# RWKV-7 chunk inverse: the transposed inverse of two heads in four is kept in the other half of the partitions

## The reference, cut to what matters

```python
def step(S, inp):
    r_t, w_t, k_t, v_t, a_t, b_t = inp
    sa = jnp.einsum('bhvk,bhk->bhv', S, a_t)
    S = S * w_t[:, :, None, :] + sa[..., None] * b_t[:, :, None, :] + v_t[..., None] * k_t[:, :, None, :]
    y = jnp.einsum('bhvk,bhk->bhv', S, r_t)
```

## Time and profile before

| | us |
|---|---|
| median of 3 runs (lowest to highest) | 1478.87 (1474.42 to 1480.12) |
| the profiled execution's own time | 1475.65 |
| its span | 1473.7 |
| PE busy in the span | 1400.1 (95%) |
| PEld, DVE, ACT, POOL busy | 1151.5, 869.1, 696.3, 39.7 |

### The profile page before, as it was taken

One profiled execution on the slowest core, in us unless ns is written; L12 is line 12 of the kernel. 1 busy time (PEld: TensorE's weight loads), 2 busy tenths in 40 slices (PEclk: granted clock), 3 DMA queues, 4 the chain that ended last, 5 costly groups with the idle time before them and its releaser, 6 DMA issues.

```text
span 1473.7 us, 22686 instructions
## 1 busy us (share of the span) xinstructions
PE 1400.1 (95%) x8406; PEld 1151.5 (78%) x8406; DVE 869.1 (59%) x1250; ACT 696.3 (47%) x1094; POOL 39.7 (3%) x41
## 2 busy tenths in 40 slices
PE   6999999889799999999899999999999999899998
PEld 5888878667688878888787688867888887788887
DVE  4555558684664555544775566755555567455554
ACT  5444456455455454434543433315544465464442
POOL 0000000000000000000000000110000011000000
PEclk9999999889899999999898999999999999999999
DMA  8655637335255555565353001203655652255553
GB/s 274 213 171 180 198 119 232 121 128 184 101 175 172 156 168 178 196 203 194 121 172 100 30 3 31 78 29 115 200 183 187 217 177 66 73 181 181 182 188 109
DMA packets 145515, 220.40 MB, mean 150 GB/s; under 512 B 16752, under 2 KB 65150, under 8 KB 145312
## 3 DMA queue, kind: packets, MB, share of 16 engines
q1 hardware_dynamic: 145440, 219.36, 45.5%
HBM read 218.26 MB, written 1.05 MB: 149 GB/s over the span
## 4 chain that ended last, share of the span: by engine, by line
PE 85%; DVE 8%; ACT 4%; issue 2%; POOL 0%; DMA 0%; SPq 0%; ACTq 0%; DVEq 0%
PE gp L287 12%; PE gp L289 11%; PE gp L288 11%; PE acc L287 11%; PE acc L289 11%; PE acc L288 11%; PE tp L904 1%; PE gp L2415 1%; DVE sb_w_lo L276 1%; PE acc L2431 1%; PE acc L2428 1%; ACT sb_w_hi L260 1%; ACT sb_xa_hi L451 1%; ACT sb_arena L401 1%; PE acc L2166 1%
## 5 line engine op out<-in xcount | busy, mean ns | idle before, releaser
L276 DVE TENSOR_TENSOR sb_w_lo<-sb_raw,sb_w_hi 128x1024 fp32r<-128x1024 f32 x380 | 454.5, 1222 | 224.8 <-ACT sb_w_hi L260 222.5
L260 ACT ACTIVATE sb_w_hi<-sb_raw 128x1024 fp32r<-128x1024 f32 x380 | 390.2, 1058 | 222.4 <-PE acc L289 104.8
L287 PE MATMUL gp<-sb_w_hi,sb_xa_hi 128*128 128x512 f32 (+2 forms) x752 | 299.3, 398 | 12.1 <-DVE sb_xa_lo L458 9.9
L289 PE MATMUL gp<-sb_w_lo,sb_xa_hi 128*128 128x512 f32 (+2 forms) x752 | 292.3, 389 | 0.0
L288 PE MATMUL gp<-sb_w_hi,sb_xa_lo 128*128 128x512 f32 (+2 forms) x752 | 292.0, 388 | 0.0
L287 PEld LDWEIGHTS gp<-sb_w_hi,sb_xa_hi 128*128 128x128 f32 x752 | 143.3, 191 | 45.5 <-issue 11.1
L289 PEld LDWEIGHTS gp<-sb_w_lo,sb_xa_hi 128*128 128x128 f32 x752 | 142.9, 190 | 29.5
L288 PEld LDWEIGHTS gp<-sb_w_hi,sb_xa_lo 128*128 128x128 f32 x752 | 143.5, 191 | 27.2 <-issue 0.5
L287 PE MATMUL acc<-sb_w_hi,sb_mid_hi 128*128 128x512 f32 x408 | 159.1, 390 | 0.0
L289 PE MATMUL acc<-sb_w_lo,sb_mid_hi 128*128 128x512 f32 x408 | 158.9, 389 | 0.0
L288 PE MATMUL acc<-sb_w_hi,sb_mid_lo 128*128 128x512 f32 x408 | 158.7, 389 | 0.0
(11 more groups left out here) (410 smaller groups left out, 1785.7 us busy)
## 6 DMA issues: line engine op xcount, KB each, us to landing
sb_raw<-in_ffn_w SPq DMA_DIRECT2D x264, 256.0 KB, 4.3
sb_raw<-in_mlp_w SPq DMA_DIRECT2D x256, 256.0 KB, 2.9
sb_raw<-in_w_in SPq DMA_DIRECT2D x72, 256.0 KB, 3.5
sb_raw<-in_a_w_rkv SPq DMA_DIRECT2D x48, 256.0 KB, 4.0
sb_raw<-in_xattn_w_kv SPq DMA_DIRECT2D x32, 256.0 KB, 3.2
sb_raw<-in_w_out SPq DMA_DIRECT2D x16, 256.0 KB, 5.9
sb_raw<-in_xattn_w_q SPq DMA_DIRECT2D x16, 256.0 KB, 2.9
sb_raw<-in_xattn_w_o SPq DMA_DIRECT2D x16, 256.0 KB, 3.0
```

Of the source, the lines that this page charges most:

```text
L260: A.e.activation(w_hi[:, s], raw[:, r], ACT.Copy).then_inc(hi_done, 1)
L276: V.e.tensor_tensor(w_lo[:, s], raw[:, r], w_hi[:, s].bitcast(F32), ALU.subtract).then_inc(lo_done, 1)
L287: e.matmul(dst, xh, wh, start=start, stop=False)
L289: return e.matmul(dst, xh, wl, start=False, stop=stop)
```

## The change

The data of odd heads (m = 1 and 3) are crossed: their `z_buf` and `y_inv` of half c are kept in the other half of the partitions, while `x_inv` and `mt` stay. `gp` and `tp` become two views of one tensor `low_banks`, in which the two banks of a stream lie side by side. Z and the new X go to the two banks of `low_banks` (even heads in one, odd heads in the other), Y to the two banks of `acc`. The order within a group is `tiles()` in place of `halves()`. The reads of PSUM by `act_z` and `dve_xy` take two banks in one instruction, with the same number of elements. The first level of Y is four masked copies 64x128 in place of two 64x256. After the last level the new `act_swap` (two ACT copies 64x128, SBUF to SBUF) brings the odd heads' `y_inv` back to their own half, in `z_buf`; `pe_u_first` waits for it. `act_prev` is two instructions of 128x512.

```diff
@@ act_prev
-                A.e.activation(rows(0)[:, t, :], gp[:, :, :].rearrange("p b n -> p (b n)"), ACT.Exp).then_inc(*A.one(self.prev_exp))
+                for b in range(2):
+                    A.e.activation(rows(0)[:, t, b * 512:(b + 1) * 512], gp[:, b, :], ACT.Exp).then_inc(*A.one(self.prev_exp if b else None))
@@ helpers
-                return [(m, slice(c * HALF, (c + 1) * HALF)) for m in range(4) for c in range(2)]
+            def half(self, c, other=0):
+                c = (c + other) % 2
+                return slice(c * HALF, (c + 1) * HALF)
+            def tiles(self):
+                return [(2 * j + e, c) for j in range(2) for c in range(2) for e in range(2)]
...
+            def inverse(self, s, m, c):
+                return (self.z_buf if m % 2 else self.y_inv)[s][self.half(c), m, :]
@@ pe_z
-                for m, at in self.halves():
-                    mm = T.e.matmul(gp[at, s, m * HALF:(m + 1) * HALF], self.mt[s][at, m, 0, at], self.x_inv[s][at, m, :], start=True, stop=True)
+                for m, c in self.tiles():
+                    at, e, j = self.half(c), m % 2, m // 2
+                    mm = T.e.matmul(low_banks[self.half(c, e), s, e, j * HALF:(j + 1) * HALF], self.mt[s][at, m, 0, at], self.x_inv[s][at, m, :],
+                                    start=True, stop=True)
@@ pe_xy
-                    for m, at in self.halves():
-                        mm = T.e.matmul(acc[at, s, 512 + m * HALF:512 + (m + 1) * HALF], self.y_inv[s][at, m, :], self.z_buf[s][at, m, :], start=True, stop=True)
+                    for m, c in self.tiles():
+                        e, j, there = m % 2, m // 2, self.half(c, m % 2)
+                        mm = T.e.matmul(low_banks[self.half(c), s, e, j * HALF:(j + 1) * HALF], self.y_inv[s][there, m, :], self.z_buf[s][there, m, :],
+                                        start=True, stop=True)
...
-                for m, at in self.halves():
-                    mm = T.e.matmul(acc[at, s, m * HALF:(m + 1) * HALF], self.z_buf[s][at, m, :], self.y_inv[s][at, m, :], start=True, stop=True)
+                for m, c in self.tiles():
+                    e, j, there = m % 2, m // 2, self.half(c, m % 2)
+                    mm = T.e.matmul(acc[there, s, e * 512 + j * HALF:e * 512 + (j + 1) * HALF], self.z_buf[s][there, m, :], self.y_inv[s][there, m, :],
+                                    start=True, stop=True)
@@ pe_u_first (pe_u_second reads self.inverse(s, m, 1) in the same way)
+                T.e.wait_ge(self.swapped, 2 * (u + 1))
                 T.e.wait_ge(self.rhs_done, u + 1)
                 for m in range(4):
-                    mm = T.e.matmul(acc[0:HALF, s, m * HD:(m + 1) * HD], self.y_inv[s][0:HALF, m, :], self.rhs_buf[s][0:HALF, m, :], start=True, stop=True)
+                    mm = T.e.matmul(acc[0:HALF, s, m * HD:(m + 1) * HD], self.inverse(s, m, 0), self.rhs_buf[s][0:HALF, m, :], start=True, stop=True)
@@ act_swap, new
+            def act_swap(self, A, u):
+                s = u % 2
+                A.e.wait_ge(self.inv_y_done[s], LEVELS * (u // 2 + 1))
+                for c in range(2):
+                    A.e.activation(self.z_buf[s][self.half(c), 1::2, :], self.y_inv[s][self.half(c, 1), 1::2, :], ACT.Copy).then_inc(*A.one(self.swapped))
@@ act_core
                     self.act_rhs(A, u - 1)
+                    self.act_swap(A, u - 1)
                     self.act_z(A, u, 1)
@@ dve_first
                 for c in range(2):
-                    at = slice(c * HALF, (c + 1) * HALF)
-                    V.e.copy_predicated(self.y_inv[s][at], levels[at, 0, 0, :].unsqueeze(1).to_broadcast([HALF, 4, HALF]),
-                                        self.mt[s][at, :, 0, at]).then_inc(*V.one(self.first_y))
+                    at = self.half(c)
+                    for e in range(2):
+                        V.e.copy_predicated(self.y_inv[s][self.half(c, e), e::2, :], levels[at, 0, 0, :].unsqueeze(1).to_broadcast([HALF, 2, HALF]),
+                                            self.mt[s][at, e::2, 0, at]).then_inc(*V.one(self.first_y))
```

More of the change, by code:

```diff
@@ L206, in build @@
         acc = ps("acc", [P, NT, D])
-        gp = ps("gp", [P, NT, 512])
-        tp = ps("tp", [P, 2, 512])
+        low_banks = ps("low_banks", [P, 2, 2, 512])
+        gp, tp = low_banks[:, :, 0], low_banks[:, :, 1]
         def const(name):
@@ L1862, in __init__ @@
                 self.rhs, self.rhs_done, self.u, self.u_done = sem(n + "rhs"), sem(n + "rhs_done"), sem(n + "u"), sem(n + "u_done")
-                self.carry, self.carry_done = sem(n + "carry"), sem(n + "carry_done")
+                self.carry, self.carry_done, self.swapped = sem(n + "carry"), sem(n + "carry_done"), sem(n + "swapped")
                 self.y, self.y_done, self.state, self.state_done = sem(n + "y"), sem(n + "y_done"), sem(n + "state"), sem(n + "state_done")
@@ L2342, in place, with by_bank, of_banks @@
                 return u % 2, u // 2, u // self.GROUPS, u % self.GROUPS
-            def halves(self):
-                return [(m, slice(c * HALF, (c + 1) * HALF)) for m in range(4) for c in range(2)]
+            def half(self, c, other=0):
[3 more added lines that the diff above has]
+                return [(2 * j + e, c) for j in range(2) for c in range(2) for e in range(2)]
+            def by_bank(self, x):
+                return x.rearrange("p (j e) d -> p e j d", e=2)
+            def of_banks(self, x):
+                return x.rearrange("p e (j d) -> p e j d", d=HALF)
+            def inverse(self, s, m, c):
+                return (self.z_buf if m % 2 else self.y_inv)[s][self.half(c), m, :]
             def stream_banks(self, s):
@@ L2421, in pe_xy @@
                 if n == 0:
-                    T.e.wait_ge(self.first_y, 2 * (u + 1))
+                    T.e.wait_ge(self.first_y, 4 * (u + 1))
                 else:
@@ L2468, in pe_u_second @@
                 for m in range(4):
-                    mm = T.e.matmul(acc[HALF:P, s, m * HD:(m + 1) * HD], self.y_inv[s][HALF:P, m, :], self.rhs_buf[s][HALF:P, m, :], start=True, stop=True)
+                    mm = T.e.matmul(acc[HALF:P, s, m * HD:(m + 1) * HD], self.inverse(s, m, 1), self.rhs_buf[s][HALF:P, m, :], start=True, stop=True)
                 mm.then_inc(*T.one(self.u))
@@ L2583, in act_z @@
                 A.e.wait_ge(self.z[s], LEVELS * (u // 2) + n + 1)
-                A.e.activation(self.z_buf[s].rearrange("p m d -> p (m d)"), gp[:, s, 0:256], ACT.Copy).then_inc(*A.one(self.z_done[s]))
+                A.e.activation(self.by_bank(self.z_buf[s]), self.of_banks(low_banks[:, s, :, 0:2 * HALF]), ACT.Copy).then_inc(*A.one(self.z_done[s]))
+            def act_swap(self, A, u):
[3 more added lines that the diff above has]
+                    A.e.activation(self.z_buf[s][self.half(c), 1::2, :], self.y_inv[s][self.half(c, 1), 1::2, :], ACT.Copy).then_inc(*A.one(self.swapped))
             def act_rhs(self, A, u):
@@ L2635, in act_core @@
                 self.act_rhs(A, last)
+                self.act_swap(A, last)
                 self.act_u(A, last, 0)
@@ L2640, in four @@
             def four(self, mask):
-                return mask.unsqueeze(1).to_broadcast([P, 4, HALF])
+                return mask.unsqueeze(1).unsqueeze(1).to_broadcast([P, 2, 2, HALF])
             def dve_masks(self, V, u):
@@ L2668, in dve_xy @@
                     V.e.wait_ge(self.x[s], (LEVELS - 1) * i + n + 1)
-                    V.e.copy_predicated(self.x_inv[s], self.four(levels[:, 1, n + 1, :]),
-                                        acc[:, s, 512:768].rearrange("p (m s) -> p m s", m=4)).then_inc(*V.one(self.x_done[s]))
+                    V.e.copy_predicated(self.by_bank(self.x_inv[s]), self.four(levels[:, 1, n + 1, :]),
+                                        self.of_banks(low_banks[:, s, :, 0:2 * HALF])).then_inc(*V.one(self.x_done[s]))
                 V.e.wait_ge(self.inv_y[s], LEVELS * i + n + 1)
-                V.e.copy_predicated(self.y_inv[s], self.four(levels[:, 0, n + 1, :]),
-                                    acc[:, s, 0:256].rearrange("p (m s) -> p m s", m=4)).then_inc(*V.one(self.inv_y_done[s]))
+                V.e.copy_predicated(self.by_bank(self.y_inv[s]), self.four(levels[:, 0, n + 1, :]),
+                                    self.of_banks(acc[:, s, :].rearrange("p (e n) -> p e n", e=2)[:, :, 0:2 * HALF])).then_inc(*V.one(self.inv_y_done[s]))
             def dve_carry(self, V, u):
```

## The result

The changed kernel takes **1487.52 us** (median of 6 executions, 1475.95 to 1490.9) where the kernel before takes 1479.41 (6 executions, 1474.42 to 1480.59): ratio **1.005**, 95% interval 1.0027 to 1.0072. In ten more executions, beside 31 of the kernel before, it took 1482.3 (1476.81 to 1488.89) against 1477.61 (1473.73 to 1481.58), ratio 1.0029 [1.0007, 1.005]. The forecast was 1477.9 in a range of 1470.5 to 1484.5, with 0.85 on "no change". The first median lies above the range, and the change makes the kernel slower.

The account below looks back on a forecast made before the run. It took a mixed chain, 85% through PE, as the bound. Gains of z and x groups on PE, mostly paid back to DVE copies and ACT's swap, summed to -0.98 us: 1478.87 to 1477.9, range 1470.5 to 1484.5.

Parts of the forecast that it names:

- no change: The case that the whole kernel's time stays within 0.5% (7.4 us), chance 0.85.
- part (a): From pairs to z(u-1,4): DVE's four masked copies take 1.28 us, +0.34 a round; shorter PE groups beside them gain nothing.
- a last sign of error: Last item listed as proving the forecast wrong: a granted clock below 1.00 in the rounds; no size given.
- the -1.0 of the sum: All terms over the whole kernel together: -0.98 us.
- z and x: These PE groups, on four quadrants, take 0.46 us in place of 0.68, gaining 0.22 each.
- rival 1's smaller form: In z and x groups, a 25 ns floor between starts: gain only 0.09 a group, 1481.9 us; chance 0.02.
- y kept 0.67: y groups on PE still use two quadrants and gain 0; forecast at 0.63 to 0.68 us.
- The swap: Behind act_rhs on ACT: two copies take 0.65 us, u_first starts at 1.23 behind rhs, carry 0.51 later a round.
- The rounds' sum: Round terms: +0.34 DVE copies, -0.44 z and x, +0.51 swap, -0.22 z(u,2); x(u,2) -0.22 in rounds 4 to 7.
- the -1.10 of the sum: In unit 0, five z and x groups on the chain gain 0.22 us each, -1.10 together.
- Rivals: Alternatives: z and x quadrants don't overlap (0.12), ACT's swap is free (0.05), PE passes between groups earlier (0.10).
- The swap costs nothing: Rival: if ACT ran the swap ahead of rhs, each round is 0.95 better, 1471.2 us; chance 0.05.

Follow-up runs that it names:

- e7: Changed kernel with weight loads held until after round 7 and a wait added in rhs of unit 6 (stop of 1.90 us); 1489.65 us, ratio 1.0084.
- e13: e7 with every z and x group issued twice in round 7 and on the levels behind it; 1480.5 us, ratio 1.0026.
- e6: Kernel before with weight loads held until after round 7; 1477.29 us, ratio 0.9995.
- e1: Changed kernel run again with no edit; 1482.3 us, ratio 1.0029 to the kernel before.
- e5: Changed kernel with the two swap copies moved ahead of act_rhs on ACT; 1480.04 us, ratio 1.002 to the kernel before.
- e2: Changed kernel with its shorter groups written again where TensorE waits anyway; 1480.32 us, ratio 1.0039 to the kernel before.
- e3: Changed kernel with weight loads held until after round 7; 1480.6 us, ratio 1.0008 to the kernel before.
- e4: Kernel before with one wait added in rhs of unit 6, stopping TensorE for 1.89 us; 1481.78 us, ratio 1.0031.
- e8: Changed kernel with swap copies ahead of act_rhs and weight loads held until after round 7; 1473.17 us, ratio 0.9977 to the kernel before.
- e12: e8 run again without a new edit; 1473.38 us, ratio 0.9962 to the kernel before.
- e15: e8 with the wait added in rhs of unit 6 (stop of 1.90 us); 1476.3 us, ratio 0.9998 to the kernel before.
- e14: The straight layout of e11 with heads 2 and 3 left out of the z and x groups; gave no time.
- e9: e7 with groups written again where TensorE waits, as in e2; 1489.21 us, ratio 1.0068 to the kernel before.
- e11: e10 with weight loads held until after round 7 and the wait added in rhs of unit 6; 1484.28 us, ratio 1.004 to the kernel before.
- e10: Kernel before with only the two swap copies and the wait for them added, no crossing; 1481.97 us, ratio 1.0025.

## Why the prediction was wrong

- **The failed step is in part (a):** PE's groups beside DVE "get shorter for nothing: the next thing late is DVE". I priced freed TensorE time by the chain alone. The clock is 1.00 in the row of round 4 and stood in the prediction as a last sign of error, but no term and no rival had it as a mechanism. In the runs the freed time isn't free. Where PE stops in round 7, the changed kernel is at a granted clock of 0.50 for 27.3 us (its trace, and e7), and for 6.8 with the groups issued twice (e13).
- **What it cost.** Set side by side at the same instructions, the trace of the changed kernel is 1.6 us behind that of the kernel before ahead of unit 0, 11.4 at 990 us and 14.8 at the end. So 9.9 us lie where the change acts, for the -1.0 of the sum. The other 4.9 lie in code that the change leaves alone, in which the clock has low stretches that come and go, in the kernel before too: its trace is at 0.50 for 58.4 us of the span in all, that of e6 for 75.1, and e6's traced execution took 1481.61. The same difference between unit 0 and 990 us is 7.8 us in e1, 5.0 in e5 and 9.7 in e7, but 0.9 in e2, 3.0 in e3, 3.9 in e4, -0.3 in e6, 3.5 in e13 and -3.6 in e8 and e12.
- **The stop** (1.75 us in the trace) was in no step either. No term has DMA, and the row of round 4 shows 3 GB/s. From 957 to 959 us, in round 7, it is 391 GB/s, in the kernel before 405, and beside these loads a transfer of instructions starts at record 5800 of PE, with the loads held at 5714 to 5730.
- **z and x:** 0.46 us, as forecast. No run shows the 25 ns between starts of rival 1's smaller form: (0.46 - 0.218) / 15 is 16 ns, as in a_mat of the kernel before. y kept 0.67: right.
- **Part (a), +0.34:** 1.28 us for four copies, right. The rows before had no copy whose output alone moves. The second and the fourth of the four are such, and they start 0.32 and 0.33 us behind the one ahead, the third, whose input alone moves, 0.33. The two 128x128 copies ahead of them, which stay in place, start 0.20 apart.
- **The swap:** two copies in 0.64 for the 0.65 taken. u_first starts 1.17 us behind rhs for 1.23. carry is 2.28 behind rhs, not 2.45: PE saw act_u's end 0.04 later, where I took 0.14. The delay was 0.33 a round, not 0.51.
- **The rounds' sum:** +0.3 and -0.3 us over rounds 1 to 6; my terms gave +0.57 and -0.09. Unit 0 took 13.50 for 14.59, the -1.10 of the sum. From the pairs of unit 0 to those of unit 7 the trace has 120.42 us for 121.44, 1.0 less where the terms gave 0.6 less. Up to round 7 the mechanism of the sum was right.
- **Rivals:** none happened. "The swap costs nothing" named the right remedy: e5 and e8 are that order of ACT.

What stays open: how often the stop on "issue" comes in the executions that have no trace, and why the same 1.9 us stop is followed by 27.3 us at a granted clock of 0.50 in e7 and by none at that place in e15. That less work alone, with straight groups, makes the fall long isn't shown: the counterpart of e13 (e14) gave no result.

## What to carry to other kernels

Where a change shortens matmuls that something else covers, look at the granted clock of that stretch and of the next 30 us, and ask what would happen if TensorE stopped there for 2 us: the saving can be paid back several times over in work at the lower clock. Here a sum of -1.0 us met 27.3 us at a granted clock of 0.50, and 9.9 us more between unit 0 and 990 us. An inserted copy goes ahead of a copy that waits for later data, not behind it; here that order of two lines was worth 0.3 to 0.6 us a round. And a burst of weight loads at 400 GB/s is worth trying at another place than beside hundreds of short TensorE instructions: here no trace with the loads behind round 7 has the stop of 0.7 to 2.0 us on "issue".

## What the runs showed of the hardware that I had not expected

- TensorE stops for 0.7 to 2.0 us on "issue" at the same record of the program in four traces (changed, e1, e5, e10), each time while the loads' packets took 103.8 to 106.1% of the time of the DMA engines (over the stop). In them it goes on 1.34 to 1.51 us after a transfer of instructions has landed. With the loads moved the stop is gone (e3, e7, e8, e12).
- After an added stop of 1.9 us the granted clock went to 0.50, 0.5 us behind its end in e4 and e9, 1.3 to 1.4 us in e7, e11 and e13; in e15 it didn't. Behind a stop of either kind it was back at 1.00 after 3.4 to 6.8 us with the old amount of work (e4, e10, e11, e13), and after 23.9 to 30.7 us with the crossed groups (changed, e1, e5, e7, e9), in the changed kernel across stretches in which PE was busy 16.00 of 16 us, with output gates of 128x512 among them.
- The fall was shorter with more work around and behind the stop, 6.8 us in e13 with the groups issued twice for 27.3 in e7, and not with work added mostly ahead of it, 30.7 us in e9. PE can be busy by the profile for 16.00 of 16 us and stay at 0.50 (changed kernel, 970 to 986 us).
